# First norm of a two-block transformer: wide rows copied first, a weight tile rounded earlier, unread products on TensorE

## The reference

```python
def _rms_norm(x, g):
    xf = x.astype(jnp.float32)
    y = xf * lax.rsqrt(jnp.mean(xf * xf, axis=-1, keepdims=True) + EPS)
    return (y * g.astype(jnp.float32)).astype(x.dtype)

def _modulate(x, g, shift, scale):
    return _rms_norm(x, g) * (1 + scale) + shift
...
    aq, ak, av, bq, bk, bv = _split_even(hx @ w_in)
```

## Time and profile before

| | |
|---|---|
| median of three executions | 1367.02 us (1365.75 to 1367.78) |
| the profiled execution's own time | 1364.35 us |
| its span | 1362.3 us |
| PE busy in the span | 1322.2 us (97%) |
| DVE busy | 989.8 us (73%) |
| ACT busy | 667.7 us (49%) |
| POOL busy | 197.2 us (14%) |
| TensorE clock granted, mean | 0.995 |

### The profile page before, as it was taken

How to read it: one execution, slowest core, us unless ns; L and a number is a source line. 1 busy time by engine, 2 the same in 40 slices (tenths; PEclk the granted TensorE clock), 3 DMA queues, 4 the chain that set the end, 5 groups by cost and what they waited for, 6 DMA issues and landing times. The chain is left out here.

```text
span 1362.3 us, 25041 instructions
## 1 busy us (share of the span) xinstructions
PE 1322.2 (97%) x9430; PEld 1167.0 (86%) x9430; DVE 989.8 (73%) x1724; ACT 667.7 (49%) x1354; POOL 197.2 (14%) x280
## 2 busy tenths in 40 slices
PE   7999999999999999999999899999999999999987
PEld 6786779888888888898896899999999978999967
DVE  6697778999887877978339565565665986765874
ACT  4327744621623315344238564466455466465573
POOL 0101213000000000123006600000220016020043
PEclk8999999999999999999999999999999999999999
DMA  8783134466895958824320345655475433454511
GB/s 307 271 240 117 48 109 140 155 217 230 304 310 198 302 202 301 296 95 140 97 90 1 111 153 162 208 183 171 139 260 170 148 120 109 146 178 165 164 43 47
DMA packets 67665, 233.15 MB, mean 171 GB/s; under 512 B 7280, under 2 KB 12400, under 8 KB 67312
## 3 DMA queue, kind: packets, MB, share of 16 engines
q1 hardware_dynamic: 67568, 231.84, 50.3%
HBM read 230.76 MB, written 1.05 MB: 170 GB/s over the span
## 5 line engine op out<-in xcount | busy, mean ns | idle before, releaser
L946 DVE TENSOR_TENSOR wlo<-raw,whi 128x1024 fp32r<-128x1024 f32 (+1 forms) x284 | 347.1, 1223 | 165.9 <-ACT whi L596 160.3
L596 ACT ACTIVATE whi<-raw 128x1024 fp32r<-128x1024 f32 (+1 forms) x284 | 296.4, 1044 | 239.7 <-PE ps L1687 238.0
L1685 PE MATMUL ps<-Hh,whi 128*128 128x256 f32 (+1 forms) x896 | 303.2, 338 | 3.9 <-DVE wlo L946 1.9
L1687 PE MATMUL ps<-Hh,wlo 128*128 128x256 f32 (+1 forms) x896 | 299.8, 335 | 0.0
L1686 PE MATMUL ps<-Hl,whi 128*128 128x256 f32 (+1 forms) x896 | 299.7, 335 | 0.0
L1685 PEld LDWEIGHTS ps<-Hh,whi 128*128 128x128 f32 x896 | 169.1, 189 | 27.1 <-issue 5.2
L1687 PEld LDWEIGHTS ps<-Hh,wlo 128*128 128x128 f32 x896 | 168.9, 189 | 19.1
L1686 PEld LDWEIGHTS ps<-Hl,whi 128*128 128x128 f32 x896 | 169.1, 189 | 18.2
L1685 PE MATMUL ps<-HIDh,whi 128*128 128x256 f32 (+1 forms) x536 | 176.5, 329 | 0.0
L1685 PE MATMUL ps<-Gh,whi 128*128 128x256 f32 x624 | 176.0, 282 | 0.4 <-DVE Gl L1153 0.4
L1686 PE MATMUL ps<-HIDl,whi 128*128 128x256 f32 (+1 forms) x536 | 176.3, 329 | 0.0
(11 more groups left out here) (261 smaller groups left out, 2064.9 us busy)
## 6 DMA issues: line engine op xcount, KB each, us to landing
raw<-wall SPq DMA_DIRECT2D x270, 512.0 KB, 4.2
aring<-aall SPq DMA_DIRECT2D x144, 512.0 KB, 4.8
raw<-wall SPq DMA_DIRECT2D x14, 384.0 KB, 3.1
AL<-ali SPq DMA_DIRECT2D x14, 192.0 KB, 5.8
X<-xin SPq DMA_DIRECT2D x2, 1024.0 KB, 7.0
BI<-rpb SPq DMA_DIRECT2D x4, 512.0 KB, 10.1
out<-X SPq DMA_DIRECT2D x4, 256.0 KB, 2.4
cst<-const SPq DMA_DIRECT2D x1, 960.0 KB, 7.3
```

What stands on the lines that cost most here:

```text
L596: act.activation(whi[:, slot, 0:n], raw[:, slot, 0:n], ACT.Copy).then_inc(sem("w_hi"), 1)
L946: dve.tensor_tensor(wlo[:, slot, 0:n], raw[:, slot, 0:n], whi[:, slot, 0:n].bitcast(F32), ALU.subtract)\
L1685: pe.matmul(o, a[0], b[0], start=first, stop=False)
L1687: return pe.matmul(o, a[1], b[0], start=False, stop=last)
```

## The change

Six edits, all in the start.

1. PE gets three products of 128x256 ahead of its first wait for constants. They read `RC`, which DVE clears first (a memset and the semaphore `zeroed`).
2. PE gets `keep(6, 7)` before `ada_mm(0)`, `keep(4, 7)` before `sums`, `keep(3, 4)` between `ada_turn(0)` and `spread`, and `keep(3, 4)` after `spread`.
3. DVE copies wide rows 0 and 1 to `SB`, before the additions of squares. Before, row 0 was copied after them, and row 1 by ACT.
4. ACT rounds weight tile 0 right after the squares, before its copy of row 2 and `ada_rows(0)`.
5. ACT rounds tiles 1, 2 and 3 before `first_hi` of tile 0 of the norm. Before, tiles 2 and 3 came after it.
6. DVE makes the low part of weight tile 0 before `ada_cols(0)` and no longer after it.

```diff
             for k in range(KT):
                 act.wait_ge(sem(f"x_landed{k // 4}"), 16)
                 act.activation(first_square(k), X[:, k, :], ACT.Square).then_inc(sem("sq"), 1)
-            for v in (2, 1):
-                act.wait_ge(sem("sb_ps"), v + 1)
-                act.activation(SB[:, v, :], ps[:, 2 * v:2 * v + 2, :].rearrange("p b n -> p (b n)"), ACT.Copy)\
-                   .then_inc(sem("sb_rows"), 1)
-                if v == 2:
-                    ada_rows(0)
-            for u in range(2):
+            split_hi(0, 0, 1)
+            act.wait_ge(sem("sb_ps"), 3)
+            act.activation(SB[:, 2, :], ps[:, 4:6, :].rearrange("p b n -> p (b n)"), ACT.Copy).then_inc(sem("sb_rows"), 1)
+            ada_rows(0)
+            for u in range(1, FIRST):
                 split_hi(u, u, 1)
             first_hi(norms["l0a"], 0)
-            for u in range(2, FIRST):
-                split_hi(u, u, 1)
...
+            dve.memset(RC[:, 0, :], 0.0).then_inc(sem("zeroed"), 1)
             dve.memset(scs[:, :, :], 0.0).then_inc(sem("dve_link"), 1)
...
+            for v in range(2):
+                dve.wait_ge(sem("sb_ps"), v + 1)
+                dve.tensor_copy(SB[:, v, :], ps[:, 2 * v:2 * v + 2, :].rearrange("p b n -> p (b n)"))\
+                   .then_inc(sem("sb_row0"), 1)
             for k in range(1, KT):
                 dve.wait_ge(sem("sq"), k + 1)
...
-            dve.wait_ge(sem("sb_ps"), 1)
-            dve.tensor_copy(SB[:, 0, :], ps[:, 0:2, :].rearrange("p b n -> p (b n)")).then_inc(sem("sb_row0"), 1)
             variance(norms["l0a"])
+            split_lo(0, 0)
             ada_cols(0)
-            split_lo(0, 0)
...
+            pe.wait_ge(sem("zeroed"), 1)
+            for _ in range(3):
+                pe.matmul(ps[:, 7, 0:N], RC[:, 0, 0:P], RC[:, 0, :], start=True, stop=True)
             pe.wait_ge(sem("cst_landed"), 16)
...
+            keep(6, 7)
             ada_mm(0)
+            keep(4, 7)
             sums(norms["l0a"])
             pe.wait_ge(sem("sb_rows"), 1)
             ada_turn(0)
+            keep(3, 4)
             spread(norms["l0a"])
-            pe.wait_ge(sem("sb_rows"), 2)
-            pe.wait_ge(sem("sb_row0"), 1)
+            keep(3, 4)
+            pe.wait_ge(sem("sb_row0"), 2)
```

More of the change, by code:

```diff
@@ L1442, in _ @@
             dve.wait_ge(sem("tables_landed"), 16)
-            dve.wait_ge(sem("sb_rows"), 2)
-            dve.wait_ge(sem("sb_row0"), 1)
+            dve.wait_ge(sem("sb_rows"), 1)
+            dve.wait_ge(sem("sb_row0"), 2)
             for i in range(1, L0_FM):
```

## The result

The changed kernel takes 1368.78 us (median of 12 executions, 1366.69 to 1372.08), the kernel before 1365.85 us on the same chip (12 executions, 1364.14 to 1369.19). The ratio is 1.0020, 95% interval [1.0012, 1.0028]: slower by 2.7 us, between 1.6 and 3.8. The profiled execution took 1368.64 us, with a span of 1366.8. The forecast was +1.3 us and no change that can be measured. The sign is right and the time lies in the range; the size is too small by half, and the case that came true is the first half of the slow rival. The whole interval lies above 1, so the shift can be measured after all, with twelve executions of each.

A forecast was written before the change was run, and what follows sets the result against it. Three chains (norm, DVE, DMA) lead to PE's step 1 at 26.45 us; its first product moves to 27.75, so 1367.02 + 1.30 = 1368.3 us, no measurable change; range 1365.5 to 1370.5.

The forecast's parts named there:

- The sign: Whole kernel: slower, by +1.30 us.
- the first half of the slow rival: Wide rows: three first products leave full clock at 9.5 us; sums 4.1 late, +2.7 us; whole slow rival's chance 0.20.
- The place: First product of step 1 on PE, at 26.45 us before the change, forecast at 27.75.
- the chain of waits: Start: additions end 15.65, PE's queue releases sums 16.62, scaling 19.80, DVE's low part ends 27.69, step 1 at 27.75.
- The first three products. What they may bring is the clock: PE before the wide rows: full clock at 6.5 us, not 9.5; wide rows end at 11.28, not 12.57.
- On DVE the low part of tile 0 (1.2) runs in POOL's time: nothing: DVE between sums and scaling: this 1.2 us instruction, moved earlier, costs nothing.
- the 5.07 assumed: DVE from the norm's scaling to the low parts of tiles 2 and 3: 5.07 us without a gap.
- I let the shift at 26.45 reach the end whole: From step 1 to the end: the whole shift, +1.30 us, persists; the 0.55 us DMA wait at 47.73 moves along.
- the fast rival: Step 0: only the clock counts; step 1 at 25.1 us, -1.3 us, total 1365.7; chance 0.15.
- The fear that the clock falls again: PE near 19.8 us: half clock returns, as at about 1163 us before; +2.8 us, within the slow rival's 0.20.
- the Trainium skill's rule on transposes: PE's four transposes: they do not count as clock activity like products, so would not help hold the clock.

The follow-up runs named there:

- e1: Changed kernel without the three first products on PE and the memset they read; ratio 1.0012 to the kernel before.
- e5: Changed kernel with the three first products reading ones, not zeros; one execution, 1368.74 us.
- e6: Changed kernel with five first products, not three, reading ones, not zeros; one execution, 1366.51 us.
- e11: Changed kernel with five first products, not three, still reading zeros; ratio 1.0008 to the kernel before.
- e8: Changed kernel with DVE waiting for POOL's root before making the low part of weight tile 0; ratio 1.0007 to the kernel before.
- e4: Kernel before with all the change's unread products, but the old orders on DVE and ACT; ratio 1.0001 to the kernel before.
- e2: Changed kernel without the ten unread products ahead of the sums (keep(6, 7) and keep(4, 7)); ratio 1.0015 to the kernel before.
- e3: Changed kernel with none of its unread products, only the changed orders on ACT and DVE; ratio 1.0027 to the kernel before.
- e7: Kernel before with only six unread products added, two before the transposes and four after; ratio 0.9996 to the kernel before.
- e9: Kernel before with the 960 KB tables' DMA issued after unit 15 of aring, not unit 11; ratio 1.0002 to the kernel before.
- e10: Kernel before with six unread products in step 0 and the tables' DMA issued after unit 15, not 11; ratio 0.9998 to the kernel before.

## Why the prediction was right or wrong

The place, the sign and the chain of waits hold. The change puts DVE's additions and PE's sums back, PE's own queue decides by a little over DVE (18.23 against 17.30; forecast 16.62 against 15.65), step 0 runs at full clock, and PE then waits for DVE's low part at step 1. The size is wrong: 3.64 at step 1 and not 1.30, 2.34 too little. It comes from two terms.

The first is the step "The first three products. What they may bring is the clock": I took the rise at 6.5 us, by carrying 4.8 us over from the wide rows to the three products. It came at 9.95, a little beyond the upper bound that I had set (9.5). That moved the end of the wide rows from 11.28 to 12.70, 1.42 us (a little less than the later rise alone would give, since the fast products take 0.22 and not the 0.24 of my sum); the ten products and `ada_mm(0)` took 5.53 and not 5.34, and together the sums moved from 16.62 to 18.23, 1.61 us. e1 and e5 show that the three do nothing, e6 and e11 that five do it, and that the sums are then near where I put them. The 4.8 us were one draw, besides: from the first wide product to the rise it took 3.0 to 5.6 us in the six kernels without products in front.

The second is "On DVE the low part of tile 0 (1.2) runs in POOL's time: nothing". It does run in POOL's time, but started before the root it delays it. From sums to scaling I had 3.18 us, and it took 4.04: 0.86. e8 shows that it is this instruction, and e4 that it is its start ahead of the root. The trace of before had it already, in a norm near the end that I did not read (its timeline, columns as above; below it the same root in the changed kernel, where it started first):

```profile
1015.61 1.21 DVE L946 TENSOR_TENSOR wlo<-raw,whi 128x1024 fp32r<-128x1024 f32 x1
...
1015.84 1.55 POOL L1547 TENSOR_TENSOR VR<-VR,mhalf 128x2 f32<-128x2 f32 x1 [1.51 <-DVE VR L1051]
...
1018.69 0.71 POOL L1546 TENSOR_TENSOR VR<-VR,mhalf 128x2 f32<-128x2 f32 x1 [1.84 <-DVE VR L1047]
...
1018.96 1.22 DVE L942 TENSOR_TENSOR wlo<-raw,whi 128x1024 fp32r<-128x1024 f32 x1 [0.42 <-ACT whi L596]
```

There the root took 1.55 behind the start of the subtraction, and 0.71 ahead of it. The Trainium skill, page "GPSIMD Engine Reference", section "1. Specifications", says that GpSimd's SBUF interfaces are shared with VectorE and that it contends with DVE instructions with two SBUF inputs; the subtraction is one, and the trace agrees with 1.85 against 1.01.

The two make 2.47. DVE's own stretch was 0.09 shorter than the 5.07 assumed, and the start of step 1 0.04 nearer, which leaves 2.34.

"I let the shift at 26.45 reach the end whole" was half right. In the changed kernel the shift goes from 3.64 to 3.72 behind the loop. In e2, e3 and e4 it shrinks by 0.7 to 0.8 at the DMA wait, which they do not have. For gains it is wrong: e7 won 0.65 at step 1 and had nothing at 55 us. By that, the fast rival's -1.3 us would have been lost at unit 15 too; no run had its case.

The fear that the clock falls again, by the earlier trace rows, did not come true in the changed kernel; in e2, with the last six products alone, it fell during PE's wait of 2.45 us. Six products were enough in e7, where PE waited 0.56 us at that place. Of the Trainium skill's rule on transposes that the prediction cites no run here shows anything: in the changed kernel and in e7 they stand between unread products.

That the forecast for the time came within 0.5 us (1368.3 against 1368.78) is luck. It stood on 1367.02, a median of three, and the twelve executions have 1365.85: this 1.17 took up most of the 1.4 that the shift was too small by. And the shift at step 1 in one profiled execution gives +3.6, the timed runs +2.7 [1.6, 3.8]; e9 suggests why, as the profiled kernel before stood better at step 1 than it may on average.

## What to carry to other kernels

Unread products that hold TensorE's clock cost nothing only inside a wait that is longer than they are (e7); ahead of a short one they become the wait, and a warm-up must be tested for the rise and not for the count: three did nothing, five took the wide rows from 8.0 to 5.6 us. Before a wide two-input subtraction on VectorE is put "into GpSimd's time", see which of the two starts first and whether anything waits for GpSimd: behind the subtraction the root took 1.85 us, ahead of it 1.01. And before time is won at the start, find the first wait for a transfer behind it: a gain can be given back there, as in e7, and e10, with the order of the transfers changed too, kept it at 55 us. Both are one execution, and in neither do the timed runs show a gain.

## What the runs showed of the hardware that I had not expected

- The granted clock reads 1.00 from the first microsecond, while the wide rows run at half rate (0.43 us a product, 0.22 later) until 7.7 to 10.4 us in all eleven kernels that do not have five products in front. At the start of a program the rate of the products tells the clock, and the table does not.
- Three products of 128x256 from 1.18 us on and a gap of 0.19 to 0.35 us left the rise at 8.4 to 10.4 us in five kernels (from the starts of the wide rows' products), and none at all had it at 7.7 to 10.4 in six; five without a gap had it at 4.2 on ones and 4.75 on zeros.
- The root on POOL, four elements a partition: 1.85 us beside a subtraction of 128x1024 on DVE that started 0.24 us before it, 1.01 without it or with the root starting first (0.33 us ahead and more); with two elements 1.55 and 0.71. Where the subtraction started first, the root ended 0.6 to 0.9 us after it.
- Two executions with the same program up to 30 us (before and e9) differ by 1.9 us at 28 us, by when `X` lands and when the half clock ends.
